# Issuing one of three weight streams of an expert stage from the scalar engine's queue

## The reference, cut to what matters

```python
for e in range(N_EXPERTS):
    y = (silu(t @ w_gate[e]) * (t @ w_up[e])) @ w_down[e]
    out = out + combine[:, e:e + 1] * y
```

## Time and profile before

| | |
|---|---|
| median of 3 runs | 1373.66 us (1371.73 to 1375.25) |
| profiled execution, its own time | 1372.92 us |
| its span, first to last instruction | 1371.3 us, mean granted TensorE clock 0.994 |
| PE busy | 1349.1 us, 98% of the span |
| DVE busy | 1078.9 us, 79% |
| ACT busy | 924.8 us, 67% |
| bytes of SP's queue (q1) | 416.19 MB, 195568 packets |
| bytes of ACT's queue (q10) | 0.00 MB, 2 packets |
| bytes of POOL's queue (q0) | 14.42 MB, 4848 packets |
| loads of the experts' weights | 3 x 112, 1024 KB each |

### The profile page before, as it was taken

How to read it: one execution, slowest core, us unless ns; L and a number is a source line. 1 busy time by engine, 2 the same in 40 slices (tenths; PEclk the granted TensorE clock), 3 DMA queues, 4 the chain that set the end, 5 groups by cost and what they waited for, 6 DMA issues and landing times.

```text
span 1371.3 us, 17378 instructions
## 1 busy us (share of the span) xinstructions
PE 1349.1 (98%) x7295; PEld 1136.9 (83%) x7296; DVE 1078.9 (79%) x710; ACT 924.8 (67%) x755; POOL 127.8 (9%) x145
## 2 busy tenths in 40 slices
PE   8999999999999999999999999999999999999997
PEld 7878999989777888888888888888888888888886
DVE  5746444456567888988888888888888888888996
ACT  6665333354667777777777777777777777777774
POOL 3310000012116600000000000000000000000010
PEclk9999999999999999999999999999999999999999
DMA  9845555646438999999999999999999999999993
GB/s 307 238 141 179 189 186 187 200 126 216 142 123 278 390 381 368 396 385 380 384 392 371 378 393 374 375 391 387 366 381 395 372 370 396 391 363 374 396 396 139
DMA packets 200501, 431.78 MB, mean 315 GB/s; under 512 B 9697, under 2 KB 45793, under 8 KB 200418
## 3 DMA queue, kind: packets, MB, share of 16 engines
q1 hardware_dynamic: 195568, 416.19, 83.9%
q0 software_dynamic: 4848, 14.42, 2.8%
q10 hardware_dynamic: 2, 0.00, 0.0%
HBM read 418.58 MB, written 7.35 MB: 311 GB/s over the span
## 4 chain that ended last, share of the span: by engine, by line
PE 96%; DVE 2%; ACT 1%; issue 0%; DVEq 0%; ACTq 0%
PE ps L1237 93%; PE ps L1505 2%; PE ps L1487 0%; PE ps L1371 0%; ACT w_high L677 0%; PE ps L1264 0%; DVE h_td L955 0%; ACT L730 0%; DVE xr L1138 0%; DVE w_low L930 0%; DVE hT_both L968 0%; ACT work_a L699 0%; ACT cacc L807 0%; ACT hT_both L715 0%; PE ps L1337 0%
## 5 line engine op out<-in xcount | busy, mean ns | idle before, releaser
L930 DVE TENSOR_TENSOR w_low<-raw,w_high 128x2048 fp32r<-128x2048 f32 x390 | 899.6, 2308 | 206.3 <-ACT w_high L677 206.0
L677 ACT ACTIVATE w_high<-raw 128x2048 fp32r<-128x2048 f32 x390 | 747.2, 1916 | 270.5 <-PE ps L1237 269.8
L1237 PE MATMUL ps<-w_high,hT_both 128*128 128x512 f32 (+1 forms) x1920 | 600.0, 390 | 0.0
L1237 PEld LDWEIGHTS ps<-w_high,hT_both 128*128 128x128 f32 x1920 | 359.7, 188 | 71.5
L1237 PE MATMUL ps<-w_low,hT_both 128*128 128x512 f32 (+1 forms) x960 | 370.8, 386 | 0.0
L1237 PE MATMUL ps<-w_high,act_both 128*128 128x512 f32 x1072 | 343.1, 391 | 1.8 <-DVE act_both L1130 1.8
L1237 PEld LDWEIGHTS ps<-w_high,act_both 128*128 128x128 f32 x1072 | 202.1, 189 | 43.8 <-DVE act_both L1130 2.1
L1237 PEld LDWEIGHTS ps<-w_low,hT_both 128*128 128x128 f32 x960 | 181.2, 189 | 34.7
L1237 PE MATMUL ps<-w_low,act_both 128*128 128x512 f32 x536 | 209.4, 391 | 0.0
L1237 PE MATMUL ps<-hT_both,w_high 128*128 128x256 f32 x960 | 176.6, 284 | 1.1 <-DVE hT_both L968 1.1
L1237 PEld LDWEIGHTS ps<-hT_both,w_high 128*128 128x128 f32 x960 | 151.5, 193 | 2.4 <-issue 2.0
(11 more groups left out here) (254 smaller groups left out, 650.7 us busy)
## 6 DMA issues: line engine op xcount, KB each, us to landing
raw<-in_moe_w_gate SPq DMA_DIRECT2D x112, 1024.0 KB, 7.8
raw<-in_moe_w_up SPq DMA_DIRECT2D x112, 1024.0 KB, 7.7
raw<-in_moe_w_down SPq DMA_DIRECT2D x112, 1024.0 KB, 7.9
raw<-in_w_in SPq DMA_DIRECT2D x13, 1024.0 KB, 6.0
raw<-in_dense_w_gate SPq DMA_DIRECT2D x11, 1024.0 KB, 5.4
raw<-in_dense_w_up SPq DMA_DIRECT2D x11, 1024.0 KB, 5.3
raw<-in_dense_w_down SPq DMA_DIRECT2D x11, 1024.0 KB, 4.9
raw<-in_w_out SPq DMA_DIRECT2D x8, 1024.0 KB, 9.2
```

The source lines that it names most:

```text
L677: act.activation(w_part[0][:, s % PART_RING, :], raw[:, s % RAW_RING, :], ACT.Copy).then_inc(w_high_done, 1)
L930: dve.tensor_tensor(w_part[1][:, q, :], raw[:, r, :], w_part[0][:, q, :], ALU.subtract).then_inc(w_low_done, 1)
L1237: return pe.matmul(out_, lhsT, rhs, start=start, stop=stop, skip_group_check=True)
```

## The change

The loads of the up projection's slots move from SP's program to ACT's, for the groups 2 to 55 (54 groups, 108 loads). The up slots of groups 0 and 1, all gate and down slots, and everything outside the expert stage stay with SP. In step k, ACT issues the two up slots of group k + 2, which are the slots t + 8 and t + 9: the first right after high(t + 3), the second right after high(t + 4). Each waits for the same count of `w_low_done` that SP waited for. The passes for overfull experts (where `i` is not None) keep their loads on SP.

```diff
@@ sync engine, expert_steps
                     if after is not None:
-                        gate_up(s + 6 * n, *after, i, per)
+                        gate_up(s + 6 * n, *after, i, per, (0, 1) if i is not None or n == 0 else (0,))
                     down(s + 6 * n + (4 if after is not None else 0), e, g, i, per)
@@ scalar engine, expert_steps
+                def load_up(k, j):
+
+                    if i is None and k + 2 < experts * EG:
+                        e_, g_ = divmod(k + 2, EG)
+                        new = s + 6 * (k + 1) + 2 + j
+                        act.wait_ge(w_low_done, new - RAW_RING + 1)
+                        act.dma_start(raw_slot(new, 4), eu_v[e_, :, 4 * j:4 * j + 4, 512 * g_:512 * g_ + 512]).then_inc(landed[new % RAW_RING], 16)
...
                     if not last:
                         high(t + 3, i, per_s)
+                        load_up(k, 0)
                         act.wait_ge(w_used, at(i, per_s, t + 2))
                         act.activation(silu_t, ps[:, 0, :], ACT.Silu).then_inc(silu_done, 1)
                         high(t + 4, i, per_s)
+                        load_up(k, 1)
                         high(t + 5, i, per_s)
```

## The result

The changed kernel takes 1378.14 us (median of 20 runs, 1372.02 to 1381.22) against 1373.52 us (1371.66 to 1375.28): a ratio of 1.0033, 95% interval 1.0024 to 1.0042. That is 4.6 us more, and the runs spread over 9 us where those of before spread over 4. The profiled execution took 1380.2 us, span 1378.6, 7.3 us more than the one of before.

What follows compares the result with a forecast made beforehand. PE was taken to bound the kernel, with transfers some 5% below; 1372.92 us + 0 - 0 = 1372.9, and 1374 for the median, which stands 0.7 above that execution; range 1369 to 1384.

Steps and rivals of the forecast that it cites:

- within 0.3%: Whole kernel: a difference under 4.1 us, which can't be told from none; chance 0.75.
- The forecast that all is hidden: Expert stage: ACT's issues and the moved loads cost PE nothing, 1371 to 1377 us; chance 0.67.
- the rival of the late gates: Expert stage: gate loads land late behind overtaking up loads, 2 to 5 us, 1376 to 1379; chance 0.12.
- PE bounds the stage, and the change can give nothing: Expert stage, 440 to 1338 us: PE is always busy, so removing SP's 108 issues is worth 0.
- What ACT's issues cost: Two issues in each of 54 steps, 0.52 us each, fit in ACT's idle 0.73 to 1.60 us: cost 0.
- my two readings of ACT: An issue on ACT runs beside the ACTIVATE ahead, or only after it ends, 0.18 us late; both hidden.
- Two queues and the late gates: Expert stage: even sharing turns a gate's landing L into 2L - 4.7; 0 at the median, 2.5 us at the end.
- slot t + 13: The last gate slot before an up pair, used 12.8 us after its issue; late only above L = 8.75 us.
- That it limits itself: Late gates: PE's slip delays later issues too, so total loss is about the landings' rise above 8.75 us, 2.5 us.
- Lost throughput: All 54 steps: interleaved queues move less, costing time from a 5% loss; 8% ends at about 1401; chance 0.08.

Runs made afterwards that it cites:

- experiment 5: The change with POOL's expert-stage transfers cut from 512 KB to 8 KB each, compared with the kernel before: 1374.91 us, ratio 1.0006.
- experiment 2: The kernel before, SP issuing all loads, plus 4 KB copies on ACT at the change's places, each waiting for the one before: 1448.9 us, ratio 1.0557.

## Why the prediction was right and where it was not

The time of 1378.1 lies in the range of 1369 to 1384; the point, 1374, and the 75% on "within 0.3%" did not foresee a loss of 0.33%, which is at that limit. The forecast that all is hidden (1371 to 1377, 0.67) did not come true. What came is nearest to the rival of the late gates (1376 to 1379, 0.12), in another form than I gave it; that the range held owes something to luck.

- **PE bounds the stage, and the change can give nothing:** right. The steps between the late loads are 16.79 us.
- **What ACT's issues cost:** right. They took 0.37 us, SP's price, not the 0.52 taken. A usual step after, ACT and then DVE:

```profile
802.10 1.92 ACT L677 ACTIVATE w_high<-raw 128x2048 fp32r<-128x2048 f32 x1 [0.78 <-PE ps L1248]
803.20 0.37 ACTq L830 DMA_DIRECT2D raw<-in_moe_w_up  x1
804.76 0.60 ACT L843 ACTIVATE work_a<-ps 128x512 f32<-128x512 f32 x1 [0.74 <-PE ps L1248]
...
800.87 2.29 DVE L941 TENSOR_TENSOR w_low<-raw,w_high 128x2048 fp32r<-128x2048 f32 x1 [0.43 <-ACT w_high L677]
```

The issue begins 0.04 us after the low half that it waits for (803.16), in the midst of a running ACTIVATE, and the idle time before the silu is 0.74 us as before. Of my two readings of ACT the first holds: the issue does not wait for the end of the ACTIVATE ahead of it.

- **Two queues and the late gates:** this is the step that failed, in its size and in its form. I doubled what was left of a median landing by even sharing, found slot t + 13 the only one at risk and priced it at 2.5 us, at the end of the stage. Measured are late loads of both streams, up (4) more than gate (3), anywhere in the stage, at a median that hardly moved (7.5 to 7.7 us from 500 to 1300 us; up alone 7.9, where I had said under 7.5) but a longest landing that went from 10.4 to 15.6. The profiled execution lost 7.5 us this way. The step that failed is to treat a load as one piece whose remaining time doubles. A load lands with the last of its sixteen parts, and in the late ones it was a part, on one DMA engine, that shared its turns with loads needed later: 15 of 16 parts at 9.5 us, the last at 15.6. I had also left out that PE's clock falls behind a long wait. The rule of the Trainium skill that I set beside it (DMA: Bandwidth & Descriptors, "Queues, rings and completion order"), that each DMA engine takes turns between the queues with work, agrees with this trace: a packet of 84 ns every 0.24 us, beside packets of 0.16 us. What I drew from it, one landing for all sixteen alike, does not.
- **That it limits itself:** not borne out. Each episode comes on top of the last, because the cause is not a backlog that grows slowly: between 540 and 590 us the median landing of SP's loads was 10.1 us and the longest 15.1, in the next 50 us 7.6 and 8.8. The kernel before has a high median between 540 and 590 us too (9.1), but a longest of 9.6.
- **Lost throughput:** not the cause. The stage moved 380 GB/s instead of 383, but that is PE's 893.10 busy us of 898, and between the late loads the pace was PE's.

Open: what puts one DMA engine behind the others and so starts an episode. Three of the four lie within 25 us of POOL's transfers, in the worst one POOL's queue had 35.5% of the engines for 3 us, and experiment 5 loses less.

## What to carry to other kernels

A stream of loads that is used in a fixed order, from a ring with little time to spare, belongs in one queue; here it did not matter which engine issued it, since its wait was met when the engine came to it. A second queue kept the median landing and lengthened the tail, because a DMA engine that is behind gives half its turns to loads that are needed later. So compare the time from issue to use with the longest landing, not the median. Where the DMA engines are near their limit and the issuing engine is idle anyway, splitting a stream had nothing to give and the order to lose.

## What the runs showed of the hardware

- A copy of 4 KB in a queue of its own took 5.4 us (4.7 to 7.2) to land beside a queue that keeps the engines at a share of 1.04; a second queue is no express lane.
- An issue of 1 MB on ACT takes 0.37 us, as on SP, and runs beside an ACTIVATE; six of them in a step of 16.79 us cost nothing. An unmet wait of such an issue holds all that follows: 75 us in experiment 2.
- One DMA engine with work in two queues took a packet of each in turn: a 2 KB packet of 84 ns started every 0.24 us, with 0.16 us, the time of a 4 KB packet, between. The last of a load's sixteen signals came up to 6.1 us after the fifteenth.
- An idle time of PE of 2.5 us was followed by some 3 us at the 1.2 GHz level, 1.6 us more lost.
